# U and V rows of an expert with one gather of 8192 bytes a partition, in the latent tiles of a two-layer trunk

## The reference

```python
D, PEER_HEADS, PEER_TOPK, PEER_N_KEYS = 1024, 8, 16, 128     # 16384 experts a layer

def peer_ffn(h, w_q, subkeys, u_tab, v_tab):
    q = (x @ w_q).reshape(n_tok, PEER_HEADS, 2, PEER_KEY_DIM // 2)
    s = jnp.einsum('thpd,hpnd->thpn', q, subkeys)
    half_s, half_i = lax.top_k(s, PEER_TOPK)
    cand = half_s[:, :, 0, :, None] + half_s[:, :, 1, None, :]
    best_s, best_i = lax.top_k(cand.reshape(n_tok, PEER_HEADS, -1), PEER_TOPK)
    ...
    experts = i1 * PEER_N_KEYS + i2                  # 8 x 16 = 128 experts a token
    gates = softmax(best_s)
    act = gelu(einsum('td,tkd->tk', xt, take(u_tab, e, axis=0))) * g
    return einsum('tk,tkd->td', act, take(v_tab, e, axis=0))

def trunk_layer(x, cond, p, lambda_init, cache):
    ...
    mix, ctx_tensors = token_mixing(modulate(x, sh1, sc1), p, lambda_init, cache)
    x = layer_norm_affine(ALPHA * x + g1 * mix, ...)
    ffn = peer_ffn(modulate(x, sh2, sc2), ...)
    return layer_norm_affine(ALPHA * x + g2 * ffn, ...), ctx_tensors
```

## Time and profile before

| what | us |
|---|---|
| median of 3 runs | 3278.56 |
| lowest and highest run | 3271.46, 3279.97 |
| span of the profiled execution, first to last instruction | 3182.4 |
| median less span | 96.2 |
| PE busy in the span | 2560.7 (80%) |
| DVE busy | 2120.2 (67%) |
| POOL busy | 1699.9 (53%) |
| ACT busy | 733.8 (23%) |
| moved by DMA | 1071 MB, 337 GB/s over the span |

### The profile page before, as it was taken

The page is one execution under the profiler, slowest core; times in us unless marked ns, Lnnn a source line. Parts: engine busy times, 40 slices in busy tenths (PEclk is TensorE's granted clock), DMA queues, the critical chain, the costliest instruction groups (busy, mean ns, idle before and its releaser), DMA issues.

```text
span 3182.4 us, 30101 instructions
## 1 busy us (share of the span) xinstructions
PE 2560.7 (80%) x8920; PEld 1447.1 (45%) x8920; DVE 2120.2 (67%) x5267; ACT 733.8 (23%) x1870; POOL 1699.9 (53%) x1540
## 2 busy tenths in 40 slices
PE   7898876989787789989897779797987766677666
PEld 2586633757463323366552235475655222232222
DVE  4633588887679993356559645877677977656665
ACT  1121112552112221143122111345111221111111
POOL 0000065555447774445557745654444777777775
PEclk9889887989898899989999989898998999888888
DMA  8856497987889999999999979897977999999997
GB/s 334 301 189 222 148 360 300 335 308 296 296 318 343 386 384 414 414 380 402 410 415 384 370 257 361 313 333 270 347 278 257 369 352 343 356 355 415 413 414 320
DMA packets 296224, 1071.03 MB, mean 337 GB/s; under 512 B 33536, under 2 KB 36352, under 8 KB 295296
## 3 DMA queue, kind: packets, MB, share of 16 engines
q0 software_dynamic: 221184, 805.40, 66.5%
q1 hardware_dynamic: 71712, 253.16, 21.3%
q10 hardware_dynamic: 3168, 10.55, 0.9%
HBM read 1065.67 MB, written 3.31 MB: 336 GB/s over the span
## 4 chain that ended last, share of the span: by engine, by line
PE 40%; DVE 21%; POOL 16%; DMA 12%; issue 10%; ACT 1%; SPq 0%; DVEq 0%; ACTq 0%; POOLq 0%
POOL ring L1687 10%; PE psum L723 9%; PE psum L813 7%; PE psum L802 6%; POOL work L1687 6%; PE psum L972 5%; DMA ring<-in_peer_v,experts 5%; DVE ring L1241 3%; PE psum L954 3%; PE psum L838 2%; DMA ring<-in_peer_u,experts 2%; PE psum L764 2%; DMA work<-in_peer_u,experts 2%; DVE work L1339 1%; DMA wring<-in_wpack 1%
## 5 line engine op out<-in xcount | busy, mean ns | idle before, releaser
L723 PE MATMUL psum<-ring,wdiag 128*128 128x512 f32 x1688 | 903.4, 678 | 337.9 <-DMA ring<-in_peer_v,experts 204.2
L1687 POOL DMA_INDIRECT ring<-in_peer_u,experts x488 | 573.1, 1174 | 941.5 <-DVE experts L1486 412.5
L1687 POOL DMA_INDIRECT ring<-in_peer_v,experts x620 | 670.8, 1082 | 361.3 <-PE psum L723 194.5
L723 PEld LDWEIGHTS psum<-ring,wdiag 128*128 128x128 f32 x1688 | 338.8, 214 | 849.9 <-issue 496.7
L1241 DVE CUSTOM_DVE_ANT_0 work<-work 128x1024 f32<-128x1024 f32 x280 | 340.0, 1226 | 197.1 <-DMA work<-in_peer_u,experts 194.4
L1241 DVE CUSTOM_DVE_ANT_0 ring<-ring,work 128x1024 f32<-128x1024 f32 x232 | 281.1, 1224 | 161.3 <-DMA ring<-in_peer_u,experts 159.3
L1687 POOL DMA_INDIRECT work<-in_peer_u,experts x280 | 294.8, 1053 | 89.5 <-issue 84.1
L1241 DVE CUSTOM_DVE_ANT_0 ring<-ring,h2a 128x1024 f32<-128x1024 f32 x256 | 304.7, 1220 | 54.7 <-DMA ring<-in_peer_u,experts 54.0
L1006 ACT ACTIVATE acts<-dots 128x2 f32<-128x2 f32 x384 | 77.8, 203 | 1055.9 <-DVE dots L1241 967.2
L723 PE MATMUL psum<-work,wdiag 128*128 128x512 f32 x492 | 257.9, 661 | 67.6 <-DMA work<-in_peer_v,experts 49.2
L813 PE MATMUL psum<-work,wring 128*128 128x256 f32 (+1 forms) x1696 | 309.1, 341 | 0.0
(11 more groups left out here) (200 smaller groups left out, 2827.6 us busy)
## 6 DMA issues: line engine op xcount, KB each, us to landing
wring<-in_wpack SPq DMA_DIRECT2D x374, 512.0 KB, 7.2
ring<-in_wpack SPq DMA_DIRECT2D x94, 512.0 KB, 5.6
ring<-in_peer_v,experts POOLq DMA_INDIRECT x620, 6.5
ring<-in_peer_u,experts POOLq DMA_INDIRECT x488, 6.5
work<-in_peer_u,experts POOLq DMA_INDIRECT x280, 6.4
work<-in_rows ACTq DMA_DIRECT2D x4, 1024.0 KB, 7.9
work<-in_peer_v,experts POOLq DMA_INDIRECT x148, 6.3
work<-in_rpb ACTq DMA_DIRECT2D x2, 1024.0 KB, 12.6
```

The source lines that it names most:

```text
L723: last = nc.tensor.matmul(psum[:, 6 + q, :], wdiag[:, SUM_NO[e] % SMALL, :], row(V_SLOT[e])[:, 512 * q:512 * (q + 1)], start=(e % KSEL == ...
L1687: pool.indirect_dma_start(row(slot), None, a[table], index).then_inc(got[slot], 16)
```

## The change

In tiles 1, 2, 4 and 5 the two gathers of an expert become one. The host writes a third table, peer_uv, whose row is the U row followed by the V row, 8192 bytes. The ring and a part of work are cut into ten double slots of 2048 words (PACKED), five in ring and five in work; the free row in the middle of ring stays unused there. One semaphore got tells of both halves. A double slot is free when the sum of its expert is done. Tiles 0 and 3 keep their separate gathers, slots and V_LAG.

The lags of the packed tiles become: Gelu 1, weights 1, diagonals 2, sum 2 steps behind the dots. The tight tiles keep 1, 2, 3 and 4. The function done_at gives each pair the step in which each part is done; at the start of a packed tile behind a tight one the lag shrinks over the first steps, so that step 4 of the tile holds three sums. The places of the steps in WORK stay as they were. The sums are still dealt to PE and DVE by vector_sums(), now by the place of the earlier step.

```diff
 TIGHT = (0, 3)
 PAIR = 2
-LAG_GELU, LAG_WTS, LAG_DIAG, LAG_SUM = 1, 2, 3, 4
-U_SMALL, V_SMALL, U_MORE, V_MORE = 4, 7, 5, 3
-MORE_AT = 15232
+def done_at(tight, packed):
+    out = []
+    for g, es in enumerate(STEP_EXPERTS):
+        n = es[0] // KSEL
+        at = g + (tight if n in TIGHT else packed)
+        out.append(max(at, out[-1] + (g == FIRST_STEP[n])) if out else at)
+    return out
+
+GELU_AT, WTS_AT, DIAG_AT, SUM_AT = done_at(1, 1), done_at(2, 1), done_at(3, 2), done_at(4, 2)
+U_SMALL, V_SMALL = 4, 7
+MORE = 5
+PACKED = RINGS // 2 + MORE
+MORE_AT = 13184
+def row_slots():
...
+            if n in TIGHT:
+                takes = [("u", e, k % U_SMALL, (k % U_SMALL,)), ("v", e, U_SMALL + k % V_SMALL, (U_SMALL + k % V_SMALL,))]
+            else:
+                c = 2 * ((k + RINGS // 2) % PACKED)
+                takes = [("uv", e, RINGS + c // 2, (c, c + 1) if c < RINGS - 1 else (c + 1, c + 2))]
...
                 def expert_step(g):                                  # PE
-                    p = g - LAG_SUM
-                    for e in range(PAIR * p, PAIR * (p + 1)):
+                    for e in [e for p in SUM_IN[g] for e in STEP_EXPERTS[p] if not by_vector(e)]:
...
-                        pe.wait_ge(got[V_SLOT[e]], 16 * V_USE[e])
+                        pe.wait_ge(got[ROW_SLOT[rows_of_sum(e)]], 16 * ROW_USE[rows_of_sum(e)])
                         pe.wait_ge(diags_made, SUM_NO[e] + 1)
...
                 def expert_step(g):                                  # ACT
-                    p = g - LAG_GELU
+                    for p in GELU_IN[g]:
+                        es = STEP_EXPERTS[p]
+                        act.wait_ge(dots_ready, es[-1] + 1)
...
-                    p = g - LAG_DIAG
+                    for p in DIAG_IN[g]:
                         act.wait_ge(wts_ready, p + 1)
...
                 def expert_step(g):                                  # DVE
-                    p = g - LAG_WTS
-                    if 0 <= p < ALL_STEPS:
+                    for p in WTS_IN[g]:
                         dve.wait_ge(gelu_ready, p + 1)
...
             def _(pool):
-                def ask_v(e):
-                    b = V_BEFORE[e]
-                    if b is not None:
-                        pool.wait_ge(rows_acc if by_vector(b) else rows_added, SUM_NO[b] + 1)
-                    ask("peer_v", e, V_SLOT[e])
...
+                def ask(what, e):
+                    key = (what, e)
+                    for was, b in ROW_BEFORE[key]:
+                        if was == "u":
+                            pool.wait_ge(dots_ready, b + 1)
+                        else:
+                            pool.wait_ge(rows_acc if by_vector(b) else rows_added, SUM_NO[b] + 1)
...
+                    if what == "uv":
+                        dst, table = pair_of_rows(key), a["peer_uv"]
+                    else:
+                        dst, table = row(what, e), a["peer_" + what]
+                    pool.indirect_dma_start(dst, None, table, index).then_inc(got[ROW_SLOT[key]], 16)
...
+                for n in range(TILES):
+                    for k in range(KSEL):
+                        e = KSEL * n + k
+                        if k % (HG * TOPK) == 0:
+                            pool.wait_ge(experts_ready, e // (HG * TOPK) + 1)
+                        if n not in TIGHT:
+                            ask("uv", e)
+                            continue
+                        ask("u", e)
+                        if k >= V_LAG:
+                            ask("v", e - V_LAG)
...
+    out["peer_uv"] = cat([out["peer_u"], out["peer_v"]], 1)
```

More of the change, by code:

```diff
@@ L70 @@
 TILE_NO = {lt: n for n, lt in enumerate(EXPERT_TILES)}
[L72 to L79 removed]
+TILES = len(EXPERT_TILES)
+ALL_EXPERTS = KSEL * TILES
 SMALL = 8
 TIGHT = (0, 3)
[L84 to L98 removed]
@@ new lines, with steps_at @@
+GELU_AT, WTS_AT, DIAG_AT, SUM_AT = done_at(1, 1), done_at(2, 1), done_at(3, 2), done_at(4, 2)
+PLACES = SUM_AT[-1] + 1
+def steps_at(when):
+    out = [[] for _ in range(PLACES)]
+    for p, g in enumerate(when):
+        out[g].append(p)
+    return out
+GELU_IN, WTS_IN, DIAG_IN, SUM_IN = steps_at(GELU_AT), steps_at(WTS_AT), steps_at(DIAG_AT), steps_at(SUM_AT)
+V_LAG = 6
+U_SMALL, V_SMALL = 4, 7
+RINGS = U_SMALL + V_SMALL
+MORE = 5
+PACKED = RINGS // 2 + MORE
+MORE_AT = 13184
+def row_slots():
+    slot, use, before, uses, last = {}, {}, {}, {}, {}
+    for n in range(TILES):
[6 more added lines that the diff above has]
+                takes = [("uv", e, RINGS + c // 2, (c, c + 1) if c < RINGS - 1 else (c + 1, c + 2))]
+            for what, e, at, cells in takes:
+                key = (what, e)
+                slot[key] = at
+                uses[at] = use[key] = uses.get(at, 0) + 1
+                before[key] = [x for i, x in enumerate(last.get(c) for c in cells) if x and x not in [last.get(c) for c in cells[:i]]]
+                for c in cells:
+                    last[c] = key
+    return slot, use, before
@@ L570, in __init__ @@
         self.end = at[0]
+        assert latent or base or self.end <= MORE_AT
 M_WORDS = 25952
```

147 lines of the change are left out of this document (64 added, 83 removed).

## The result

| kernel | median us | lowest to highest | runs |
|---|---|---|---|
| before | 3275.5 | 3271.5 to 3280.0 | 4 |
| changed | 3228.7 | 3224.6 to 3229.6 | 4 |

The changed kernel takes 0.985 of the time before, 95% interval 0.983 to 0.987: 47 us less, where I had forecast 3292, 13 more. Its profiled execution spans 3222.8 us, and this same execution took 3224.62: outside the span lie 1.8 us. If that holds for the kernel before too (it does in both later traces of it), its profiled execution, of 3182.4 us, took about 3184 and not 3279. By the two traces the change *costs* 40.4 us; by the timed runs it saves 47.

A forecast was written before the change was run, and what follows sets the result against it. Bounds: POOL's issuing in tile 4, POOL and DMA in tile 5, PE in 1205 to 1645 us. Terms -55 - 4 + 60 + 8 + 4 = +13 on the 3182.4 us span, plus 96.2, gave 3292; range 3235 to 3338.

The forecast's parts named there:

- 96.2 us lie between this and the median of 3278.56; I hold them unchanged: Whole kernel: the difference between the profiled span of 3182.4 us and the timed median stays, giving 3292 from a 3195 span.
- Stalls for the diagonal, +60: Context tile of layer 1, 1180 to 1645 us: PE's sums wait for same-step diagonals, 83 us, taken as +60 (15 to 90).
- the 20 us that I took off for this: Same context stretch: the other 20 of PE's 33 us of idle time may swallow as much of the 83 us stalls.
- Half the gathers, -55: Tiles 1, 2, 4 and 5: one gather an expert relieves POOL, saving 36 and 9 us from 2500 to 2875, 10 earlier.
- The 10 us that I booked for tiles 1 and 2: Savings from single gathers: 8 us in 1645 to 1833 us and 2 us in 1008 to 1178 us.
- The price of a gather: On POOL: a gather of 8192 bytes costs the same 1.18 us as today's, at most twice that.
- Start of tile 3, +8: Tile 3's first four U asks wait for tile 2's sums, not dots: 10.9 us against 2.8, so +8.
- Starts of tiles 1 and 4, +4: The tenth ask waits for sums that come three to a step: 0 to 8 us each, taken as 2 each.
- The end, -4: After the last dot: with V landed beside U the last sum comes 4 us sooner (0 to 6).
- One (stalls swallowed): Context stretch: DMA, not PE, sets the pace, so the stalls cost only 15 to 25 us; 3251 us, chance 0.30.
- Two (weights pushed aside): Modulation and projection items: 8192-byte packets delay weights to about 14 us, PE loses a third; +35, 3327 us, chance 0.08.
- Three (shorter lead): Tile 4: with six experts of lead, not nine, its 36 us gain does not come; +49, 3327 us, chance 0.10.

The follow-up runs named there:

- the traces on A and B: The kernel before, unchanged, profiled again on two chips: 3180.9 us on chip A, 3278.2 us on chip B.
- experiment four: The changed kernel with the sum of the packed tiles three steps behind the dots, not two: 3151.0 us on chip A, 3150.1 us on chip B.
- after_c: The changed kernel, unchanged, run once more on chip B at a later time: 3227.6 us, ratio 0.980 to the kernel before.

## Why the prediction was wrong, step by step

**The step that failed is "96.2 us lie between this and the median of 3278.56; I hold them unchanged".** I took them for time outside the span. Outside lie 1.8 us. The other 94 are the distance between the two levels of the kernel before, as the traces on A and B show it: slower gathers, with more long packets of 4096 bytes and idle DMA engines. The timed executions were at the upper level and the profiled one was at the lower; on which chips they ran is not recorded. The changed kernel has no such loss on any chip measured, so the 94 us did not stay; held unchanged they made the forecast 3292. Without them it is 3182.4 + 13 + 1.8 = 3197, to be held against the 3224.6 of the profiled execution after. That the range 3271 to 3280 of the timed runs is 9 us wide and ends 87 above 3184 was there to be read: a span 3% below runs that agree within 0.3% had to be of another kind of execution, or hide as much time outside.

**The terms of the span** came to +13; the traces show +40.

- *Stalls for the diagonal, +60.* The mis-sized term. The count of the stalls was good: I had worked out 83 us net in 51 steps, and the trace has 91.5 in 48, less the 6.2 that were there before: 85. 35 of them are plain steps with 36 us (I had 31 with 33), and 13 have a table load in between, with 56 us. What they cost is seen between the same two modulation items of PE, about 1564 matmuls, in the kernel before, after, and with the sum at three (experiment four):

```profile
1175.10:1585.80 410.70, 377.97 (x1565) 205.81 (x1565) 204.36 (x477) 114.75 (x315) 205.87 (x195) 0.95 1.01 403
```

```profile
1182.00:1675.20 493.20, 395.95 (x1564) 210.75 (x1563) 196.50 (x461) 111.78 (x312) 95.37 (x92) 0.92 0.85 325
```

```profile
1181.40:1601.10 419.70, 379.65 (x1572) 206.16 (x1571) 199.97 (x471) 111.99 (x313) 104.34 (x91) 0.96 0.96 380
```

  The stretch grew by 82.5 us, most of the 94 of tiles 1 and 2. PE's waits for diagonals grew by 79 (6.2 to 85.6). Its other idle time fell by 15 (26.5 to 11.7), so the 20 us that I took off for this were nearly right. But PE was busy 18 us longer with the same work, at a granted clock of 0.92 and not 0.95. Its rows have two speeds: within a sum a 512-column matmul follows the one before it after 0.43 us (2.4 GHz) or after 0.85 (1.2 GHz), and the slow ones are 49 of 232 here where they were 19 before. I had put this term at nothing. With the sum at three the stalls shrink to 9 us, and with them go the 18 us: 379.7 us busy at 0.96. That the lower clock comes from the stalls is read from these three rows; no run changed the clock alone.
- *Half the gathers, -55.* -45 of it was for tiles 4 and 5, which measured -57: -46 in tile 4, and -11 in tile 5, where I had said 0. Tile 4 reached the floor without the loss that I had left for two nearly full engines. Tile 5 gained, for the most part, because a packet of 8192 bytes takes 309 ns and two of 4096 take 318: 425 in place of 414 GB/s (after_c against the earlier trace rows), by my estimate 128 x (2.53 - 2.47) = 8 us on 128 experts. The 10 us that I booked for tiles 1 and 2 did not show in the dots: from the 48th of tile 2 to its last the lead of the kernel before stays at 92 to 97.
- *The price of a gather.* Taken as 1.18 us, measured 1.08 to 1.14 in tile 4 and 1.17 in tile 5. Right.
- *Start of tile 3, +8*: measured +6.9. *Starts of tiles 1 and 4, +4*: measured +1.3 at tile 4. *The end, -4*: -3.2.

**The rivals.** One (stalls swallowed) had its direction right and came nearer with 3251, by luck: its reason is refuted by experiment four, since PE does set this pace. Two (weights pushed aside) did not come: among PE's waits in 1180 to 1745 that come to 0.8 us or more in all none is for weights, though a row does go as one packet of 8192 bytes. The Trainium skill (DMA: Bandwidth & Descriptors, SWDGE vs HWDGE vs iDMA), which prefers at most 4096, gave this rival its condition. The condition held and the loss did not follow. That trace alone does not settle it, since PE's delays had lowered the DMA share to 0.87 there, as the rival itself allowed. The run with the sum at three does: its DMA share from 1180 to 1400 us is 1.00 again, and its weights land in 9.5 us, not in 14 (issues of 1200 to 1400, and all that PE waits for weights in its items at L1008):

```profile
wring<-in_wpack SPq DMA_DIRECT2D x65, 512.0 KB, 9.5
```

```profile
PE psum L1008 <- DMA wring<-in_wpack: 5.5, 4, 1.8
```

Three (shorter lead) fell with tile 4 at 2.50 us an expert.

In the step above with the table load this load lasts 1.28 us, and Gelu starts 1.32 us after the copy ends. The Trainium skill (ScalarE: Activation LUTs, What ACT_TABLE_LOAD costs) has the same 1.28 and a drain of 1.38 us besides; in this place the trace shows no room for the drain.

**What would show it.** I had named some fifty waits with 60 to 80 us (48 with 91.5), tile 2's last dot 40 to 60 us later (92), 45 to 50 us less from tile 4 on (60 with the end), POOL half busy and DMA near 400 GB/s (44%, 419). All are there, the first three larger. No sign named would have caught the 96 us.

**Open.** Why some packets of 4096 bytes are drawn out and hardly any of 8192, whether the chip itself decides it, and whether size or number of the gathers does: the experiments change both together or neither. That POOL and DMA are both full in the kernel before, and POOL is not in the changed one, is a further difference that no run takes apart.

## What to carry to other kernels

Before a sum is made against the span of a trace, compare the span with the timed runs. If they differ by more than the runs among themselves, the trace is of another kind of execution, and the difference must get a cause and a rival of its own. When a producer's lead over its consumer shrinks to the same step, work out the stalls on the bounding engine, and ask what the engine's clock does behind them: here idle time swallowed 15 us of 79, and the lower clock took 18. One step of lag, which cost nothing here, bought back 77 us. The version with the sum at three steps, which moving the weights as well did not improve, takes 3151 us, 0.8% less than the kernel before at its lower level and 4% less at its upper one.

## What was not expected of the hardware

- The same program, with 4096-byte gathers back to back, takes 3179 us on two chips and 3274 to 3290 on two others; with 8192-byte gathers it takes 3224 to 3228 us on three of the four.
- The time that a gather takes on POOL hardly depends on the length of its rows: at least 0.93 us for 4096 and for 8192 bytes a partition, with means from 0.96 to 1.18 for the one and 1.08 to 1.20 for the other in tiles 4 and 5, and 0.30 us between two of them in both kernels.
- In tile 5 8192-byte packets move 419 to 425 GB/s, 4096-byte ones 409 to 414 where they have no loss.
- A wait of PE can cost more than it lasts: behind one of 2.56 us four matmuls took 3.53 us instead of 1.98, at a granted clock of 0.54.
